# An mLSTM and convolution layer in fp32: the sample states' small products regrouped from pairs to fours, the chunk update in 257 columns, the head loops written out

## The chip, the core and the metric

The kernel runs on one core of one Trainium2 chip. The metric is the device time of one execution in microseconds. A core has TensorE for matrix products (PE, with its weight loads listed as PEld), VectorE (DVE), ScalarE (ACT), GpSimd (POOL) and SyncE (SP), which issues most DMA transfers. The engines run their own instruction streams and wait for each other by semaphores. Operands lie in an on-chip memory of 128 partitions; results of TensorE land in eight accumulator banks (out takes four of them; B4, B5, B6 and B7 are the others). The chip was seen to grant TensorE one of two clocks, 1.2 or 2.4 GHz; the profile gives it as a share of the full one.

## What is computed

One layer over 16 meta tokens and 512 prompt frames of a new stream and 8 x 16 frames of eight running streams (the "samples"), 656 columns in all. A projection of the 1024 channels gives, for each of four heads, 256 channels each of query, key, value and output gate, and the two inputs of a gated convolution branch. The part that the change touches is the chunked matrix memory. Each head runs five chunks of the prompt (16 and four times 128 frames in this kernel; the samples count as chunk 5) with a carried 256 x 256 state, and the eight samples with a state of their own each:

```python
a = b + m0[..., None]
w_state = jnp.exp(a - m)
w_intra = jnp.exp(dmat - m[..., None])
p = w_intra * jnp.einsum('bhtd,bhsd->bhts', q, k)
num = jnp.einsum('bhts,bhse->bhte', p, v) + w_state[..., None] * jnp.einsum('bhed,bhtd->bhte', C0, q)
den = jnp.sum(p, axis=-1) + w_state * jnp.einsum('bhd,bhtd->bht', n0, q)
h = num / jnp.maximum(jnp.abs(den), jnp.exp(-m))[..., None]
C1 = w_last[..., None, None] * C0 + jnp.einsum('bhs,bhse,bhsd->bhed', ws, v, k)
n1 = w_last[..., None] * n0 + jnp.einsum('bhs,bhsd->bhd', ws, k)
```

The heads' outputs are normalised, multiplied by the output gate and projected (the branch); the convolution branch is a depthwise convolution of 31 taps, a layer norm and a projection; both are gated, merged and projected, and a feed-forward block follows. All is fp32, and the states C and n of prompt and samples are outputs too.

## The kernel before

**Weight tiles.** To keep fp32 accuracy every weight tile and its right-hand side are split into a high and a low part, and TensorE forms three products. One tile of 128 output channels is one `gemm` (L374): 8 channel blocks x 3 products x 2 halves of 328 or 320 columns, 48 matmuls. For tile n, SP loads the weights to a ring of four (`ST`), ACT writes the high part (`hi`, `WH`, L325) once tile n-2 is done, DVE subtracts it (`lo`, `WL`, L329), and the gemm of tile n waits for `w_lo`. ACT then evacuates tiles (L659).

**Heads.** A head is twelve tiles, r = 0 to 11: two each of k, q, v, o and four of the convolution's gate and input. After four heads come 16 tiles of gates and branch (the "GM tiles", j = 0, 1, ...), and further stages which the change leaves alone. Right after tile r=1 of a head, TensorE transposes the normalised output of the head before (`headnorm_out`), and POOL, DVE and ACT turn it into the next operand (`epilogue_out`, `epilogue_gate`).

**Slots.** The matrix-memory work of a head stands in 14 slots on TensorE: slot 0 after tile r=7, slots 1 and 2 inside tile r=8 after 16 and 32 of its 48 matmuls, slot 3 after it, and so on to slot 12 after r=11, and 13. Tables by slot number say what stands where: `S_SLOT` (scores of chunk c, "S"), `NUM_SLOT` (numerator of c, and the update of the carried state "U" with chunk c), `TR_SLOT` (the four 128-column transposes of one sample's state, "T"), `READ_SLOT` (the product of a pair of sample states with its queries, "R") and `PAIR_SLOT` (the pair's state update, "D"). All of these are plain fp32 matmuls at L1580 (`mm`) and L1575 (`tr`); the trace holds each of them as two records. A read uses tiles of 32 output columns (128*32 in the trace), an update tiles of 32 rows (32*128), two tiles of the array at a time. In U the 256 columns of the state and the column of the normaliser are separate products (L1750 and L1752). Banks: transposes and reads in B4, scores in B5, numerators in B6, updates in B7 (a pair's second sample in B6).

**The other engines.** DVE and ACT run in program order through the same slots: DVE multiplies scores by weights (`p_ready`), adds updates to states (`update`, L1033: two a pair, `c1`; for U `ct_ready`), takes statistics of a chunk's output (`stats`), and runs `conv_input`. In heads 1 to 3 it also runs the 62 convolution taps of the head before, two instructions each (L1033, CV<-WK,cwu,CV), so many after each tile and slot by the tables `CONV_TILE` and `CONV_SLOT`. ACT copies turned states (`c0t_ready`, two buffers), copies reads and numerators, and issues the DMAs of the sample states: `c1_store` (L724), `c0_load` (L717) and, in `states_in`, the load of n (L777) and of the first four states of a head. PE's code is written out for all heads. On SP (L511), ACT (L885) and DVE (its end is L1372) head 0 is written out and heads 1 to 3 are a hardware loop.

Names in the rows: WK is the work area in which q, k, tokens by frame, states and their products lie; CV holds the convolution's output and one of the buffers for turned states; sm, mv and bst are small statistics; n0b is the samples' n; GH and GL are high and low part of the gated head output.

Of the kernel before, what the change touches and what calls it, by code (L numbers as in the profile page):

```python
# [25 lines left out]
D = 1024  # L26
# [55 lines left out]
UPDATES = []  # L82
for _s in range(NSLOT):
    if _s in NUM_SLOT and NUM_SLOT[_s] < NPC:
        UPDATES.append(("U", NUM_SLOT[_s]))
    if _s in PAIR_SLOT:
        UPDATES.append(("D", PAIR_SLOT[_s]))
# [3 lines left out]
STORE_SLOT = {_s + 1: _p for _s, _p in PAIR_SLOT.items()}  # L91
LOAD_SLOT = {_s + 2: _p + 2 for _s, _p in PAIR_SLOT.items() if _p < 2}


def pairs_done(s):
    return 2 * sum(x < s for x in PAIR_SLOT)
# [8 lines left out]
def build(nc, a):  # L105
    def sb(name, shape, dt=F32):
# [10 lines left out]
    sizes = [("q", 2 * T), ("k", 2 * T), ("qw", 2 * T), ("vn", 6 * 257), ("so", 2 * T), ("kt", 6 * 256),  # L117
             ("vt", 6 * 257), ("vws", 2 * 257), ("c0", C0RING * 512), ("c0t", 514),
             ("pt", 2 * P), ("bc", 2 * T), ("ct", 2 * 257), ("up", 2 * (PAD + TP + NB * (PAD + LB))),
             ("qm", 2 * NB * 24)]  # L120
# [7 lines left out]
    def wk(o, n):  # L128
        return WK[:, o:o + n]
# [5 lines left out]
    num = wk(off["vn"], 6 * 257).rearrange("p (c e) -> p c e", c=6)  # L135
# [46 lines left out]
    c0t = [x.rearrange("p (j e) -> p j e", j=2) for x in (CVF[:, 6 * T2:6 * T2 + 514], wk(off["c0t"], 514))]  # L182
# [64 lines left out]
    def n0_of(i, b):  # L247

        return n0t[:, :, :].rearrange("p j (b h) -> p h j b", h=HEADS)[:, bass.ds(i, 1), :, b:b + 1].rearrange(
            "p o j b -> p (o j) b")  # L250

# [193 lines left out]
    with nc.Block() as block:  # L445

        @block.sync
        def _(sp):
# [28 lines left out]
            def head_loads(i):  # L477
                first = isinstance(i, int)
# [3 lines left out]
                for r, col in enumerate(cols):  # L482
# [6 lines left out]
                    elif r == 3 and not first:  # L489

                        gated = sp.snap(ofcount(n + -1) + 1)
                        tile, src = sp.snap((i - 1) * 2), d_rows[bass.ds(i, 1), :, :]
                        tile1 = sp.snap((i - 1) * 2 + 1)
                        sp.wait_ge(sem("rows_out"), 32)
                        sp.wait_ge(sem(f"of{(n + -1).par % 2}"), gated)
                        bc_load(src)
# [3 lines left out]
                        for x, tl in enumerate((tile, tile1)):  # L500
# [9 lines left out]
            head_loads(0)  # L510
            with sp.Fori(1, HEADS) as i:  # L511
                head_loads(i)
# [58 lines left out]
        def _(g):  # L571
# [34 lines left out]
            g.wait_ge(sem("of0"), N_GM0 // 2 + 1)  # L606
            g.tensor_tensor(ln[0], CV[:, 0, :], CV[:, 1, :], ALU.add).then_inc(sem("csum"), 1)
# [17 lines left out]
        def _(act):  # L625
# [120 lines left out]
            def epilogue_out(i):  # L746

                act.wait_ge(sem("t_ct"), i + 1)
                act.wait_ge(sem("t_int"), 4 * i + 4)
# [36 lines left out]
            def head(i):  # L786

                n = N(N_HEADS0, PER_HEAD, i)
                first = isinstance(i, int)
# [9 lines left out]
                if not first:  # L799
                    states_in(i)  # L800
# [4 lines left out]
                if not first:  # L805
                    exp_weights(i)
                    epilogue_out(i - 1)
# [31 lines left out]
                else:  # L839
                    values_tok(i)  # L840
                hi(n + 8)
                evac(n + 7, two(so[:, 1, NMETA:T]), ACT.Sigmoid)
                if first:
                    values_tok(i)
                for s in range(NSLOT):
                    if s in (1, 4, 7, 10):
                        hi(n + (8 + (s - 1) // 3 + 1))
                    if s in TR_SLOT:
                        b = TR_SLOT[s]
                        act.wait_ge(sem("t_c0"), NB * i + b + 1)  # L850
                        wait(act, "t_int", 4 * i + b // 2)
# [1165 lines left out]
```

## Time and profile before

| | us |
|---|---|
| median of 3 runs | 1280.85 (1280.24 to 1281.9) |
| the profiled execution, own time | 1281.44 |
| its span | 1279.7 |
| PE busy | 1246.7 (97%) |
| PEld busy | 1160.3 (91%) |
| DVE busy | 740.0 (58%) |
| ACT busy | 390.1 (30%) |
| POOL busy | 19.8 (2%) |
| chain that ended last | PE 92%, issue 3%, ACT 2%, DVE 2% |
| DMA, mean | 91 GB/s |

The time is that of the whole execution; the span runs from the first to the last instruction in the trace, so 1.7 us lie around it. Busy shares are means over the stages. A matmul's record ends later than the next one begins, because matmuls are pipelined; the pace is read from starts. The mean granted clock was .991.

### The profile page before, as it was taken

To read this page: it belongs to the slowest core of one execution; us is meant where nothing else is said; L and a number is where in the kernel's file an instruction comes from. 1 tells how busy PE (TensorE), PEld (TensorE's weight loads), DVE (VectorE), ACT (ScalarE), POOL (GpSimd) and SP (SyncE) were. 2 spreads that over 40 slices of the span, in tenths; PEclk is the share of its full clock that TensorE was granted. 3 is DMA by queue.
4 is the path that set the end of the run, shared out by engine and by line. 5 is a ranking of instruction groups with operands and counts; after the bars stand their busy time and mean duration, and the time that the engine had idled before them with its cause. 6 is when DMAs were issued, how large, how long until landed. Compare 5 with 4: busy or idle time off the path is not lost.

```text
span 1279.7 us, 19762 instructions
## 1 busy us (share of the span) xinstructions
PE 1246.7 (97%) x7760; PEld 1160.3 (91%) x7760; DVE 740.0 (58%) x1311; ACT 390.1 (30%) x562; POOL 19.8 (2%) x37
## 2 busy tenths in 40 slices
PE   7999999989998999999999999999999999999997
PEld 7998899879987998899999998899899889989986
DVE  5633469857985798899755565443243333323453
ACT  4442243223322332231236533233123213312431
POOL 1000000000000000200000000000000000000000
PEclk8999999999999899999999999999999999999999
DMA  8253162334333423352332335012322222222221
GB/s 230 71 154 99 50 163 69 97 96 116 71 96 96 117 66 101 89 79 79 75 82 67 99 106 180 28 50 83 99 66 83 82 72 77 82 68 81 83 82 50
DMA packets 160541, 116.38 MB, mean 91 GB/s; under 512 B 13887, under 2 KB 148247, under 8 KB 160450
## 3 DMA queue, kind: packets, MB, share of 16 engines
q1 hardware_dynamic: 139122, 94.58, 27.2%
q10 hardware_dynamic: 21328, 20.55, 5.1%
q8 instruction: 62, 1.02, 0.3%
q14 instruction: 29, 0.24, 0.1%
HBM read 100.89 MB, written 14.21 MB: 90 GB/s over the span
## 4 chain that ended last, share of the span: by engine, by line
PE 92%; issue 3%; ACT 2%; DVE 2%; DVEq 0%; POOLq 0%; POOL 0%
PE out L374 42%; PE out L1580 29%; PE bank L1580 17%; PE bank L1575 4%; DVE WK L1033 1%; ACT CV L627 1%; PE out L382 1%; DVE WK L1030 0%; DVE WL L329 0%; ACT WH L325 0%; ACT L659 0%; ACT L627 0%; ACT GH L627 0%; DVE XL L1030 0%; ACT WK L659 0%
## 5 line engine op out<-in xcount | busy, mean ns | idle before, releaser
L329 DVE TENSOR_TENSOR WL<-ST,WH 128x1024 fp32r<-128x1024 f32 x137 | 168.2, 1228 | 180.7 <-ACT WH L430 100.6
L374 PE MATMUL out<-XH,WH 128*128 128x320 f32 (+1 forms) x1024 | 241.4, 317 | 9.0 <-DVE WL L329 9.0
L374 PE MATMUL out<-XH,WL 128*128 128x320 f32 (+1 forms) x1024 | 238.7, 314 | 0.0
L374 PE MATMUL out<-XL,WH 128*128 128x320 f32 (+1 forms) x1024 | 238.2, 314 | 0.0
L1033 DVE SCALAR_TENSOR_TENSOR CV<-WK,cwu,CV 128x512 f32 (+1 forms) x480 | 227.1, 541 | 0.6
L374 PEld LDWEIGHTS out<-XH,WH 128*128 128x128 f32 x1024 | 173.1, 190 | 10.3 <-DVE WL L329 9.6
L374 PEld LDWEIGHTS out<-XL,WH 128*128 128x128 f32 x1024 | 173.3, 190 | 4.6 <-issue 4.4
L374 PEld LDWEIGHTS out<-XH,WL 128*128 128x128 f32 x1024 | 173.1, 189 | 2.9 <-issue 2.7
L1030 DVE TENSOR_TENSOR WK<-WK 128x640 f32<-128x640 f32 (+7 forms) x86 | 65.1, 770 | 109.5 <-ACT WK L996 100.2
L1580 PE MATMUL out<-XH,WL 128*128 128x320 f32 (+2 forms) x512 | 119.9, 310 | 0.0
L1580 PE MATMUL out<-XL,WH 128*128 128x320 f32 (+2 forms) x512 | 119.6, 310 | 0.0
L1580 PE MATMUL out<-XH,WH 128*128 128x320 f32 (+2 forms) x512 | 119.4, 309 | 0.0
L325 ACT ACTIVATE WH<-ST 128x1024 fp32r<-128x1024 f32 x81 | 85.3, 1053 | 90.2 <-PE out L374 59.5
L1580 PE MATMUL bank<-WK 32*128 32x256 f32 (+6 forms) x536 | 99.9, 353 | 6.8 <-DVE WK L1033 6.8
L430 ACT ACTIVATE WH<-ST 128x1024 fp32r<-128x1024 f32 x56 | 58.9, 1052 | 135.3 <-PE bank L1580 68.9
L659 ACT ACTIVATE WK<-out 128x640 f32<-128x640 f32 (+1 forms) x56 | 39.8, 710 | 188.7 <-PE out L374 181.2
L1580 PEld LDWEIGHTS bank<-WK 128*128 128x128 f32 (+3 forms) x536 | 69.1, 179 | 21.6 <-issue 15.6
L1580 PEld LDWEIGHTS out<-XH,WH 128*128 128x128 f32 x512 | 86.3, 188 | 1.0
L1580 PEld LDWEIGHTS out<-XL,WH 128*128 128x128 f32 x512 | 86.3, 188 | 0.7
L1580 PEld LDWEIGHTS out<-XH,WL 128*128 128x128 f32 x512 | 86.2, 188 | 0.7
L627 ACT ACTIVATE WK<-bank 128x512 f32<-128x512 f32 (+5 forms) x100 | 43.0, 467 | 73.1 <-PE bank L1580 71.4
L1575 PE MATMUL bank<-ident,WK 128*128 128x128 f32 (+6 forms) x427 | 58.0, 275 | 6.3 <-DVE WK L1033 5.4
(219 smaller groups left out, 1608.4 us busy)
## 6 DMA issues: line engine op xcount, KB each, us to landing
ST<-in_w_in SPq DMA_DIRECT2D x65, 512.0 KB, 4.1
ST<-in_w_ff SPq DMA_DIRECT2D x64, 512.0 KB, 4.0
WK<-in_state_mlstm_C ACTq DMA_DIRECT2D x32, 256.0 KB, 3.0
o_C_sample<-WK ACTq DMA_DIRECT2D x32, 256.0 KB, 2.4
WK<-in_x_prompt SPq DMA_DIRECT2D x8, 512.0 KB, 6.4
ST<-in_w_branch_m SPq DMA_DIRECT2D x8, 512.0 KB, 4.0
ST<-in_w_branch_c SPq DMA_DIRECT2D x8, 512.0 KB, 4.1
ST<-in_w_out SPq DMA_DIRECT2D x8, 512.0 KB, 3.5
```

The costliest lines, as they stand in the source:

```text
L325: act.activation(WH[:, par % 2, :, :], ST[:, par % NSTAGE, :, :], ACT.Copy).then_inc(sem("w_hi"), 1)
L329: dve.tensor_tensor(WL[:, par % 2, :, :], ST[:, par % NSTAGE, :, :], WH[:, par % 2, :, :].bitcast(F32), ALU.subtract).then_inc(sem("w_lo"), 1)
L374: last = pe.matmul(out[s][:, h, 0:H], w[:, s, kk, :], x[:, kk, h * H:(h + 1) * H], start=(m < 2), stop=(m >= len(ms) - 2))
L382: last = pe.matmul(out[0][:, h, 0:HALF], w[:, 0, kk, :], x[:, kk, h * HALF:(h + 1) * HALF], start=(kk == 0 and w is WH and x is XH), stop= ...
L430: act.activation(WH[:, n.par % 2, :, :], ST[:, n.par, :, :], ACT.Copy).then_inc(sem("w_hi"), 1)
L627: act.activation(o, i, fn, **kw).then_inc(sem(name), 1)
L659: act.activation(o, gout(n), fn, **kw).then_inc(sem(f"of{n.par % 2}"), 1)
L1030: return dve.tensor_tensor(o, x, y, op)
L1033: return dve.scalar_tensor_tensor(o, x, s, y, op0, op1)
L1575: ins = pe.transpose(o, i, ident[0:r, 0:r])
L1580: return pe.matmul(o, l, r, start=start, stop=stop)
```

## The change

1. The eight samples of a head are worked in two rounds of four in place of four pairs. A read is eight matmuls, four tiles of 32 columns into the four row groups of B4; an update eight matmuls, four tiles of 32 rows into four banks (B6, B7, B5, B4). Turned states have four buffers in place of two. The second round's update stands in the new slot 14, in the middle of the next head's tile r=0 (after the last head: of GM tile 0); two transposes stand in new slots -2 and -1 inside tile r=7. DVE adds a round in four instructions; the second round after the normalisation of the head's output in the next head. The four stores of a round and the loads of the next four states are issued together by ACT, the stores of the second round after `hi` of the next head's tile r=2; `states_in` moves from there to behind `hi` of r=3.
2. U is two products of 257 columns (B7 and the upper part of B5), and DVE's update two instructions of 257 columns.
3. The tables of slots and taps change with it (the numerators and scores one slot later, from chunk 1 or 2 on), and `slot` is split into named functions.
4. The loops over heads on SP, ACT and DVE are written out. The buffer `num` loses its unused row; POOL waits for the last numerator before it writes into that area.

```diff
-S_SLOT = {2: 1, 4: 2, 6: 3, 8: 4, 10: 5}
-NUM_SLOT = {1: 0, 3: 1, 5: 2, 7: 3, 9: 4, 13: 5}
-PAIR_SLOT = {2: 0, 4: 1, 8: 2, 12: 3}
-TR_SLOT = {0: 0, 1: 1, 3: 2, 4: 3, 7: 4, 8: 5, 10: 6, 11: 7}
-READ_SLOT = {2: 0, 5: 1, 9: 2, 12: 3}
+S_SLOT = {2: 1, 5: 2, 7: 3, 9: 4, 11: 5}
+NUM_SLOT = {1: 0, 4: 1, 6: 2, 8: 3, 10: 4, 13: 5}
+ROUND_SLOT = {3: 0, 14: 1}
+READ_SLOT = {2: 0, 12: 1}
+TURN_SLOT = {-2: [0], -1: [1], 0: [2], 1: [3], 8: [4], 9: [5], 10: [6], 11: [7]}
+TURN_SLOT0 = {**TURN_SLOT, -2: [], -1: [0], 0: [1, 2]}
-CONV_SLOT = {s: 2 if s % 2 else 3 for s in range(NSLOT) if 0 < s < 12}
+CONV_SLOT = {1: 2, 2: 3, 4: 1, 5: 4, 6: 3, 7: 3, 8: 3, 9: 3, 10: 2, 11: 3}
...
-            head_loads(0)
-            with sp.Fori(1, HEADS) as i:
+            for i in range(HEADS):
                 head_loads(i)
...
                 hi(n + 2)
                 if not first:
-                    states_in(i)
+                    round_store(i - 1, 1)
                 evac(n + 1, two(k[:, 1, :]), scale=DH ** -0.5)
...
                 hi(n + 3)
                 if not first:
+                    states_in(i)
                     exp_weights(i)
                     epilogue_out(i - 1)
...
-                    for x in range(2):
-                        b = 2 * c + x
...
+                    for x in range(4):
+                        col = 23 + SAMPLE[4 * c + x]
+                        dve.wait_ge(sem(f"c0_in{x}"), 16 * (2 * i + c + 1))
+                        stt(c0[:, x, :, :], c0[:, x, :, :], colH[:, col:col + 1],
+                            round_bank(x).rearrange("p (j e) -> p j e", j=2), ALU.mult, ALU.add).then_inc(sem("c1"), 1)
...
             head(0)
-            with dve.Fori(1, HEADS) as i:
+            for i in range(1, HEADS):
...
                 if j == 0:
                     epilogue_norm(HEADS - 1)
+                    update(HEADS - 1, NUPD - 1)
...
+            def read_states(i, r):
+
+                pe.wait_ge(sem("c0t_ready"), NB * i + 4 * r + 4)
+                pe.wait_ge(sem("qw_ready"), i + 1)
+                for j in range(2):
+                    for g in range(4):
+                        ins = mm(B4[32 * g:32 * g + 32, 0:257], qm[:, j, g, LB * r:LB * r + 2 * LB],
+                                 c0t[g][:, j, :], j == 0, j == 1)
+                ins.then_inc(sem("t_int"), 1)
...
+                for e in range(2):
+                    for g in range(4):
+                        rows = slice(32 * g, 32 * g + 32)
+                        ins = mm(round_bank(g)[:, e * DH:e * DH + DH], w[rows, e * P:e * P + P], ktok[rows, SMP, :])
+                ins.then_inc(sem("t_upd"), 1)
...
+            def numerator(i, c):
...
+                pe.wait_ge(sem("p_ready"), 5 * i + c)
+                wait(pe, "num", 5 * i + c - 1)
+                if c == 1:
+                    pe.wait_ge(sem("c1"), NB * i + 4)
...
-                        for j in range(2):
-                            mm(B5[:, 384 + j:385 + j], ktok[0:L, c, j * P:j * P + P], w[0:L, DH:DH + 1])
-                        for j in range(2):
-                            ins = mm(B7[:, j * DH:j * DH + DH], ktok[0:L, c, j * P:j * P + P], w[0:L, 0:DH])
+                for j in range(2):
+                    ins = mm((B7[:, 0:257], B5[:, P:P + 257])[j], ktok[0:L, c, j * P:j * P + P], w)
+                ins.then_inc(sem("t_upd"), 1)
```

On PE, before, slots 12 and 13 at the end of a head read and update the last pair, and then form the samples' numerator. (`bank` are B4 to B7; `32x257` is a read, `128x256` an update, the last `128x257` the numerator.)

```order
L1580 MATMUL bank<-CV,WK 32x257 [waits c0t_ready]
L1580 MATMUL bank<-WK 32x257
L1580 MATMUL bank<-CV,WK 32x257
L1580 MATMUL bank<-WK 32x257
L1580 MATMUL bank<-WK 128x256 [waits n1,ct_ready,vws]
L1580 MATMUL bank<-WK 128x256 x3
L1580 MATMUL bank<-WK 128x257 [waits c1,n1,num,p_ready]
L374 MATMUL out<-XH,WH 128x328 [waits of1,w_lo]
```

The same place after:

```order
L1576 MATMUL bank<-WK 32x257 [waits qw_ready,c0t_ready]
L1576 MATMUL bank<-WK 32x257
L1576 MATMUL bank<-CV,WK 32x257 x2
L1576 MATMUL bank<-WK 32x257 x2
L1576 MATMUL bank<-CV,WK 32x257 x2
L1576 MATMUL bank<-WK 128x257 [waits n1,num,p_ready]
L372 MATMUL out<-XH,WH 128x328 [waits of1,w_lo]
```

The update has left the place ahead of the numerator, and with it the numerator's wait for `c1`. The update's eight matmuls follow inside the next tile:

```order
L372 MATMUL out<-XH,WH 128x328 x2
L372 MATMUL out<-XL,WH 128x328 x2
L372 MATMUL out<-XH,WL 128x328 x2
L1576 MATMUL bank<-WK 128x256 [waits p_ready,all_samples,ct_ready,num,vws]
L1576 MATMUL bank<-WK 128x256 x7
L372 MATMUL out<-XH,WH 128x328 x2
```

Behind slot 3, which updates the first round, PE has a third of tile r=9 (16 matmuls) and then slot 4, whose numerator now waits for `c1`:

```order
L1576 MATMUL bank<-WK 128x256 [waits p_ready,ct_ready,first_samples,vws]
L1576 MATMUL bank<-WK 128x256 x7
L372 MATMUL out<-XH,WH 128x328 [waits of0,w_lo]
L372 MATMUL out<-XH,WH 128x328
...
L372 MATMUL out<-XL,WH 128x328 x2
L1576 MATMUL bank<-WK 128x257 [waits c1,ct_ready,num,p_ready]
L1576 MATMUL bank<-WK 128x257 x2
L1576 MATMUL bank<-WK 128x257 [waits vws]
```

On DVE, before, a head of the loop ends with the sum and the statistics of the samples' numerator and the branch back to the `lo` of the next head:

```order
L1030 TENSOR_TENSOR WK<-out,WK 128x184
L1030 TENSOR_TENSOR WK<-out,WK 128x328
L1030 TENSOR_TENSOR WK<-WK,bank 128x257
L1254 BN_STATS bst<-WK 128x6
L1372 REGISTER_ALU
L1372 COMPARE_AND_BRANCH
```

After, the next head's `lo` (`WL<-ST,WH`) follows without a branch, and behind the normalisation (its last five instructions are `WK<-WK,sm`) stands the second round's state update:

```order
L1254 BN_STATS bst<-WK 128x6
L327 TENSOR_TENSOR WL<-ST,WH 128x1024
L1035 SCALAR_TENSOR_TENSOR sm<-WK 128x5
L1032 TENSOR_TENSOR sm<-sm,colH 128x5
...
L1184 TENSOR_SCALAR WK<-WK,sm 128x256 x5
L1035 SCALAR_TENSOR_TENSOR WK<-WK,colH,bank 128x512 x4
L1204 COPY colH<-colA 128x31
```

On ACT, after, the five loads of `states_in` (L772, L712) stand between `hi` of r=3 and the step that leads to GH, the head output's high part; before, they stood one `hi` earlier:

```order
L323 ACTIVATE WH<-ST 128x1024 [waits tile_done,ld0]
L772 DMA n0b<-in_state_mlstm_n 8x256 [waits n1_out]
L712 DMA WK<-in_state_mlstm_C 128x2x256 [waits c1_out0]
L712 DMA WK<-in_state_mlstm_C 128x2x256 [waits c1_out1]
L712 DMA WK<-in_state_mlstm_C 128x2x256 [waits c1_out2]
L712 DMA WK<-in_state_mlstm_C 128x2x256 [waits c1_out3]
...
L622 ACTIVATE WK<-bank 128x512 [waits t_int,t_ct]
L747 DMA o_C_prompt<-WK 128x2x256 [waits cp_sb]
L749 DMA o_n_prompt<-WK 128x2x1
L622 ACTIVATE GH<-WK 128x1280 [waits hmf]
```

## Rows read from the trace of the kernel before

**Rows 1.** PE's waits: engine, line, whom for; us in total, times, longest

```profile
PE out L374 <- DVE WL L329: 9.5, 4, 4.6
PE bank L1580 <- DVE WK L1033: 6.8, 4, 1.7
...
PE bank L1575 <- ACT WK L627: 1.0, 1, 1.0
```

**Rows 2.** PE timeline, tiles r=0 and r=1: start us, us, engine, line, operands, count, [idle before]

```profile
289.48 0.57 PE L374 MATMUL out<-XH,WH 128*128 128x328 f32 x2 [4.37 <-DVE WL L329]
...
404.83 0.67 PE L1580 MATMUL bank<-WK 128*128 128x257 f32 x2 [1.71 <-DVE WK L1033]
...
405.64 0.46 PE L374 MATMUL out<-XL,WH 128*128 128x328 f32 x2
...
412.25 0.47 PE L374 MATMUL out<-XH,WL 128*128 128x328 f32 x2
417.36 0.91 PE L374 MATMUL out<-XH,WH 128*128 128x328 f32 x2 [4.65 <-DVE WL L329]
```

**Rows 3.** DVE timeline behind the loop's branch, head 2 to head 3

```profile
416.08 1.22 DVE L329 TENSOR_TENSOR WL<-ST,WH 128x1024 fp32r<-128x1024 f32 x1 [9.19 <-issue]
```

**Rows 4.** Stretches: us, busy PE PEld DVE ACT POOL (count), PEclk, DMA share, GB/s

```profile
289.48:298.36 8.88, 8.88 (x49) 8.87 (x50) 6.86 (x31) 1.76 (x3) 0.00 (x0) 0.81 0.77 202
417.36:427.41 10.05, 10.05 (x49) 10.04 (x49) 6.87 (x31) 1.75 (x3) 0.00 (x0) 0.70 0.72 205
346.00:405.50 59.50, 57.79 (x380) 50.25 (x379) 49.05 (x108) 13.77 (x29) 0.00 (x0) 1.00 0.25 75
```

**Rows 5.** PE timeline, slot 2 of head 2: read, scores, update, next gemm

```profile
353.55 0.40 PE L1580 MATMUL bank<-CV,WK 128*32 128x257 f32 x1
353.55 0.40 PE L1580 MATMUL bank<-WK 128*32 128x257 f32 x1
...
354.54 0.71 PE L1580 MATMUL bank<-WK 128*128 128x128 f32 x4
...
355.18 1.13 PE L1580 MATMUL bank<-WK 32*128 32x256 f32 x8
...
356.24 0.57 PE L374 MATMUL out<-XL,WH 128*128 128x328 f32 x2
```

**Rows 6.** PE timeline, slot 3 of head 2: numerator and U, next gemm

```profile
359.19 2.78 PE L1580 MATMUL bank<-WK 128*128 128x257 f32 x14
361.62 0.65 PE L374 MATMUL out<-XH,WH 128*128 128x328 f32 x2
```

**Rows 7.** DVE timeline, slots 2 to 6 of head 2

```profile
356.48 1.41 DVE L1033 SCALAR_TENSOR_TENSOR WK<-WK,colH,bank 128x512 f32<-128x512 f32 x2 [0.90 <-PE bank L1580]
...
362.01 0.88 DVE L1033 SCALAR_TENSOR_TENSOR WK<-WK,colH,bank 128x2 f32<-128x2 f32 x2 [0.84 <-PE bank L1580]
...
363.40 1.92 DVE L1033 SCALAR_TENSOR_TENSOR CV<-WK,cwu,CV 128x512 f32 x4
...
366.38 0.28 DVE L1030 TENSOR_TENSOR WK<-bank,WK 128x128 f32<-128x128 f32 x1
...
378.99 1.02 DVE L1030 TENSOR_TENSOR WK<-out,WK 128x128 f32<-128x128 f32 x4
```

**Rows 8.** ACT's DMA issues of four sample states, written-out code of head 0

```profile
79.82 1.96 ACTq L717 DMA_DIRECT2D WK<-in_state_mlstm_C  x4
```

**Rows 9.** DVE timeline ahead of tile r=4 of head 2, then PE's start of it

```profile
305.48 1.49 DVE L1030 TENSOR_TENSOR GL<-WK,GH 128x1280 f32 x1 [2.16 <-ACT GH L627]
...
313.15 1.22 DVE L329 TENSOR_TENSOR WL<-ST,WH 128x1024 fp32r<-128x1024 f32 x1
...
315.79 0.55 PE L374 MATMUL out<-XH,WH 128*128 128x328 f32 x2
```

**Rows 10.** DVE timeline ahead of GM tile 2, then PE's start of it

```profile
546.24 1.23 DVE L329 TENSOR_TENSOR WL<-ST,WH 128x1024 fp32r<-128x1024 f32 x1
...
548.43 0.45 PE L374 MATMUL out<-XH,WH 128*128 128x320 f32 x2
```

More of the change, by code:

```diff
@@ L90 @@
 C0RING = 4
[L91 to L96, printed above, removed]
+STORE_SLOT, LOAD_SLOT = 5, 6
 CONV_TILE = {2: 7, 3: 4, 4: 7, 5: 7, 6: 7, 7: 3}
-CONV_SLOT = {s: 2 if s % 2 else 3 for s in range(NSLOT) if 0 < s < 12}
+CONV_SLOT = {1: 2, 2: 3, 4: 1, 5: 4, 6: 3, 7: 3, 8: 3, 9: 3, 10: 2, 11: 3}
 TAPS = 2 * CONV_W
@@ L250, in n0_of, with round_bank, turn_bank @@
             "p o j b -> p (o j) b")
+    def round_bank(g):
+        return (B6, B7, B5, B4)[g]
+    def turn_bank(i, b):
+        return B7 if i == 0 and b == 2 else B6 if b < 4 else B4
     def gout(n):
@@ L877, in head, with turned, round_store @@
                               ).then_inc(sem("n1_out"), 16)
+            def turned(i, s):
+                for b in (TURN_SLOT if i else TURN_SLOT0).get(s, []):
+                    act.wait_ge(sem("t_c0"), NB * i + b + 1)
+                    wait(act, "t_int", 2 * i + b // 4)
+                    if b == 0:
+                        wait(act, "cp_out", 16 * i)
+                    act.activation(c0t[b % 4][:, :, DH:DH + 1], n0_of(i, SAMPLE[b]), ACT.Copy)
+                    copy(c0t[b % 4][:, :, 0:DH], turn_bank(i, b).rearrange("p (j e) -> p j e", j=2), "c0t_ready")
+            def round_store(i, r):
+                for x in range(4):
+                    c1_store(i, 4 * r + x)
             def numer(i, c):
@@ L881, in numer @@
                 act.wait_ge(sem("t_num"), 5 * i + c)
-                copy(num[0:L, c, :], B6[0:L, 0:257], "num")
-            head(0)
-            with act.Fori(1, HEADS) as i:
+                copy(num[0:L, c - 1, :], B6[0:L, 0:257], "num")
+            for i in range(HEADS):
                 head(i)
@@ L1682, in slot, with turn @@
+            def turn(i, s):
+                for b in (TURN_SLOT if i else TURN_SLOT0).get(s, []):
+                    bank = turn_bank(i, b)
                     if b == 0:
                         pe.wait_ge(sem("kv_tok"), 8 * i + 8)
-                    wait(pe, "c0t_ready", NB * i + b)
-                    if b in (2, 4):
-                        pe.wait_ge(sem("first_samples"), 2 * i + b // 2)
-                    if b == 6:
-                        pe.wait_ge(sem("all_samples"), 2 * i + 1)
@@ new lines, in update_chunk @@
+            def update_chunk(i, c):
+                u = UPDATES.index(("U", c))
+                L = CHUNKS[c][1]
+                w = vws[0:L, (NUPD * i + u) % 2, :]
+                pe.wait_ge(sem("vws"), NUPD * i + u + 1)
+                if c == 0:
+                    wait(pe, "cp_sb", i)
+                    pe.wait_ge(sem("kv_tok"), 8 * i + 8)
+                    if i == 0:
+                        pe.wait_ge(sem("c0t_ready"), 3)
+                for j in range(2):
+                    ins = mm((B7[:, 0:257], B5[:, P:P + 257])[j], ktok[0:L, c, j * P:j * P + P], w)
+                ins.then_inc(sem("t_upd"), 1)
@@ L1718, in slot @@
+            def slot(i, s):
+                turn(i, s)
+                if s in READ_SLOT:
+                    read_states(i, READ_SLOT[s])
+                if s in S_SLOT:
+                    scores(i, S_SLOT[s])
                 if s == 11:
@@ L1770, in head @@
                         xh, xl = (XH2, XL2) if r in FRAMES_ONLY else (XH, XL)
-                        gemm(pe, n + r, xh, xl)
+                        gaps = []
+                        if r == 0 and not first:
+                            gaps = [lambda: slot(i - 1, 14)]
+                        if r == 7:
+                            gaps = [(lambda: values_by_frame(i)) if first else (lambda: slot(i, -2)), lambda: slot(i, -1)]
+                        gemm(pe, n + r, xh, xl, gaps=gaps)
                     else:
```

272 lines of the change are left out of this document (114 added, 158 removed).

## The prediction, made before the changed kernel had run

> **What bounds the kernel now.** I read the page's busy shares and the chain of waits first. PE is busy almost throughout and the chain runs through it, so a gain must either take work off PE or take away one of its waits. The list of PE's waits says which there are [rows 1]: 9.5 us in four waits for a low part of weights from DVE, of which the largest is 4.6, and 6.8 us in four waits, one a head, for a DVE update. The rest of PE's idle time before the heads' end lies in the kernel's first stage, which the change does not touch. The timeline puts places to them. The two long waits for `lo` are the starts of tile r=1 in heads 2 and 3, and the waits of 1.7 us are the samples' numerator in slot 13 [rows 2]. Then I read the slots themselves, because there the change takes matmuls away [rows 5, 6], and DVE and ACT around them, because their slack decides what the shorter slots are worth [rows 7 to 9].
>
> **The loops written out.** Ahead of the `lo` for which tile r=1 waits, DVE is idle for 9.19 us and the trace names no releaser, only "issue" [rows 3]. The instruction before it is the branch at the loop's end. So the wait belongs to the loop's return, and it comes on the two returns (heads 2 and 3) and nowhere in straight code. PE loses 4.37 and 4.65 us [rows 2]. It loses more behind that: matmuls follow each other by (412.25-405.64)/44 = .150 us [rows 2], so a tile of 48 takes 7.21, but the two tiles r=1 took 8.88 and 10.05, with granted clocks of .81 and .70 of full [rows 4]. The clock fell to its lower level in them after PE had stood still. That is 1.67 + 2.84 = 4.5 us. I take all of it as gained: 9.0 + 4.5 = **13.5**. The lower bound is 0, if straight code stalls as long at that place (a rival). SP's and ACT's loops cost PE nothing that the waits show, and I credit nothing for them.
>
> **The slot-13 wait.** Before, the last update and the numerator stand next to each other, and the numerator waits until DVE has emptied the bank. After, this update stands in the middle of the next tile and the numerator does not wait for it: 4 x 1.71 = **6.8** [rows 1, 2]. Next late there would be the numerator's inputs, the scores of slot 11, which lie more than a tile's third back; I see no new wait. The 1.0 us wait of a transpose for ACT in head 0 [rows 1] belongs to a turn that moves behind more cover: **1.0**.
>
> **Matmuls.** A read of a pair takes 354.54-353.55 = .99 us, an update 356.24-355.18 = 1.06 [rows 5]. Two tiles start at the same printed time, so the eight records run as four steps. If four tiles do the same, a round costs what a pair costs, and there are two rounds for four pairs: 2 x .99 + 2 x 1.06 = 4.1 us a head, **16.4** in four heads. This is the term with the widest bounds, 0 (four tiles run two at a time) to 16.4, and below 0 if they run one at a time; both are rivals. The row of two tiles at a time is the nearest there is, and nothing in it suggests that two is the limit: even the two starts of one step have no printed distance. U has four products of which two have one column. Numerator and U together take 361.62-359.19 = 2.43 us for 14 records [rows 6]; without the four records of one column ten wide ones are left, nine steps and the last one, which the gemm follows almost at once. A step is .25 at most (a read's .99 over four, with the change of shape at its end) and about .22 without that change: 1.98, so the U saves .45 (.2 with the larger step), x 20 updates = **9.0** (4 to 9). So matmuls give 25.4. The three new breaks inside gemms (slots -2, -1, 14) and the breaks that go about cancel; what one costs is at most the difference of the first gemm steps behind a slot and plain ones, some .1, so 1 us stays in the bounds.
>
> The Trainium skill, "TensorE: Matmul & The Clock Gate", Part 3, "Measured speedup vs the span model", gives 3.07 for four row tiles and 2.38 for three column tiles, not 4 and 3. By it a step of four would cost some 1.3 times a full one, an estimate: 1.23 us a head, and the forecast would be 5 us later. Two tiles in this trace show the full factor of two; four at a time are in no row.
>
> Gains: 13.5 + 6.8 + 1.0 + 25.4 = **46.7**.
>
> **New waits.** Now DVE has less time between the slots, and I went through them for what ends last.
> - Slot 4 (all heads): the numerator waits for the four additions of the first round, slot 3. Counted from the update's start PE arrives after 1.06 + 16 x .150 = 3.5 us. DVE starts 356.48-355.18 = 1.30 after that start, needs 1.41 for two additions and so 2.8 for four [rows 5, 7], and its signal takes another .24 (the update's end to the DVE start, 356.24 to 356.48): 4.3. Wait .7 to .8, x 4 = **2.8**. Behind PE in that wait stands the U of chunk 1, and all that follows.
> - Slot 8 (heads 1 to 3): the numerator of chunk 3 needs the weighted scores. Behind the U of slot 6 DVE has its update, the next weighting and statistics (363.40-362.01 = 1.39), three taps (six instructions at 1.92/4, 2.8), the convolution input (1.0), a `lo` (1.2) and the weighting (.28) [rows 3, 7], 6.7 with some of it overlapped; with the signal 6.7 to 6.9. PE has two thirds of a tile, 4.8, and a score and a turn of four records each (at most 355.18-354.54 = .64 each, rather .45 [rows 5]): 5.7 to 6.1. Wait .6 to 1.2, I take 1.0, x 3 = **3.0**.
> - Tile r=4 (heads 1 to 3): `states_in` now stands ahead of the copy of the head output to GH. Its four state loads take ACT 1.96 us to issue [rows 8], and DVE has already waited 2.16 for GH; `lo` of r=4 ended 1.42 before PE needed it (313.15 + 1.22 against 315.79) [rows 9]. So 1.96 - 1.42, about .6, x 3 = **1.8**. No queue is lengthened: the loads are the same ones.
> - GM tile 2: the second round's update, four additions or 2.8 us, stands ahead of its `lo`, which had .97 to spare (546.24 + 1.23, 548.43) [rows 10]: **1.8**. In heads 1 to 3 the same update stands after the `lo` of r=1, where DVE has a tile's length.
>
> Waits: 2.8 + 3.0 + 1.8 + 1.8 = **9.4**; bounds 0 (DVE has idle time that closes up) to twice that. ACT's stores and loads four at a time, SP's straight code and POOL's wait cost nothing: ACT is busy 13.77 of 59.5 us in the slots [rows 4], and the load of the next four states is issued some 14 us ahead of its turn.
>
> **Sum.** 46.7 - 9.4 = 37.3. Against the profiled execution, 1281.44, that is 1244.1; the median of the runs lies .59 below that execution, so **1243.5**. With waits of 0 it is 1234, with twice the waits 1253.
>
> **Rivals.**
> 1. Four tiles run as two pairs, so the change does not do what it says: the 16.4 us come back, **1260**. For it: no row shows more than two tiles at a time. Against it: the two show no cost of sharing.
> 2. DVE sets the pace of the slots. In the stretch of tiles r=8 to r=11 of head 2 it is busy 49.05 of 59.5 us [rows 4]. The second round's additions leave the stretch (2.8), so it keeps 46.3, and PE's stretch shrinks to about 52 by the terms above. If DVE's idle time of 10.45 stayed, because it always comes from waiting for the next slot and cannot be shifted, the stretch would be 56.7: 4.7 x 3 heads = 14, **1257**. For it: DVE's waits for PE in this stretch are many and short [rows 7]. Against it: these waits are on PE, and end earlier when PE is earlier.
>    The Trainium skill, "TensorEngine Tiling (Array Packing)", "PSUM Bottleneck", says that after such a speedup the emptying of the banks may become the bound, and to use both engines for it; here the additions of both rounds stay on DVE alone. The waits that I expect at slot 4 are of that kind.
> 3. DVE's stall of 9 us stays in straight code, since what comes after the seam is code that has not run before either way: 13.5 back, **1257**. Against it: no such gap stands in head 0's straight code, between heads or in the GM tiles, nor where the loop is left after head 3.
> 4. The other side: four tiles are run one after the other. A round would be 16 steps of .25 (the .99 over four), 4.0 us a read and 4.2 an update, two of each: 16.4 a head against 8.2 before and 4.1 in the forecast, so +49, **1292**, slower than before. It decides once a read or update of four costs more than about 3.4 us in place of 1.0. Against it stand the two reads that start at one time [rows 5].
>
> **How the numbers follow.** The forecast, 1234 to 1253 with 1243.5 as its value, gets .69; rival 1 .10, rival 2 .08, rival 3 .07, rival 4 .04; .02 lie below 1234, if DVE's earlier starts also take away waits that I did not count. The range goes from 1233 to 1259, which takes in the forecast with rivals 2 and 3, .84, and leaves out rivals 1 and 4 and what is below. Some 0.2% (2.6 us) is what a measurement can tell from no change; all cases but rival 4 are faster by far more. Faster .95, the same .01 (rival 4 in part), slower .04.
>
> **What the profile after would show.** The timeline at tile r=1 of heads 2 and 3 should have no idle time and a full clock (the stretch of 48 matmuls 7.2 us). A read or an update of four should take about 1.0 us with four records at one start. In PE's list the waits of slot 13 should be gone, and small ones stand at the numerators of slots 4 and 8 (L1576 for DVE), the gemm of r=4 (L372 for DVE's `lo`) and GM tile 2. If reads take 2 us it is rival 1; if DVE's idle time in the slots is as long as before and PE waits at most slots, rival 2; if the idle time ahead of `lo` stays, rival 3. I would be wrong in the sum if the new waits hit at more slots than I went through, the turns in r=7 above all, which now need ACT's copies earlier.

## The result, and the profile after

The changed kernel takes 1239.35 us (median of 4 runs, 1239.09 to 1240.54) against 1280.55 before (median of 4, 1279.13 to 1281.9): a ratio of 0.968 (95% interval 0.9663 to 0.9697), 41.2 us faster. The forecast was 1243.5 in a range of 1233 to 1259. The profiled execution took 1239.42 (span 1237.7), 42.0 less than before. PE is busy 1214.8 us of the span, 98%.

PE's waits after (engine, line, whom for; us in total, times, longest) answer to [rows 1]. The 9.5 and 6.8 us are gone, and so is head 0's 1.0 us wait for ACT. The three rows are new: slot 8 (0.9 in each of heads 1 to 3), GM tile 2 (1.6, with two small ones) and slot 4 (0.4 each).

```profile
PE bank L1576 <- DVE WK L1032: 2.7, 3, 0.9
PE out L372 <- DVE WL L327: 2.1, 3, 1.6
...
PE bank L1576 <- DVE WK L1035: 1.3, 3, 0.4
```

The four tiles of a read, of head 2 (PE timeline), against [rows 5]: sixteen records in four steps, 332.39-331.38 = 1.01 us for four samples where two took .99. The update of four takes 336.52-335.44 = 1.08 where a pair's took 1.06.

```profile
331.38 0.41 PE L1576 MATMUL bank<-WK 128*32 128x257 f32 x2
331.40 0.41 PE L1576 MATMUL bank<-CV,WK 128*32 128x257 f32 x2
...
332.06 0.38 PE L1576 MATMUL bank<-WK 128*32 128x257 f32 x2
332.08 0.39 PE L1576 MATMUL bank<-CV,WK 128*32 128x257 f32 x2
332.39 0.71 PE L1576 MATMUL bank<-WK 128*128 128x128 f32 x4
...
335.44 1.15 PE L1576 MATMUL bank<-WK 32*128 32x256 f32 x16
336.52 0.42 PE L372 MATMUL out<-XH,WH 128*128 128x328 f32 x1
```

Three stretches (us, busy time of PE, PEld, DVE, ACT, POOL, then PEclk, DMA share, GB/s), against [rows 4]: tile r=1 of heads 2 and 3, to the start of r=2 and with `headnorm_out` in them, and the slots of head 2. The clock is at its full level in all three.

```profile
268.48:277.14 8.66, 8.66 (x64) 8.65 (x63) 4.65 (x14) 2.91 (x4) 0.00 (x0) 1.00 0.89 257
383.22:391.88 8.66, 8.66 (x65) 8.65 (x63) 4.64 (x14) 2.91 (x4) 0.00 (x0) 1.00 0.95 273
324.68:374.54 49.86, 48.52 (x332) 43.62 (x330) 43.24 (x97) 12.92 (x26) 0.00 (x0) 1.00 0.25 72
```

At the seam of heads 2 and 3 on DVE (timeline; [rows 3] before), the low part follows the last statistics with no idle time; the branch is gone and with it the 9 us:

```profile
376.06 0.43 DVE L1254 BATCH_NORM_STATS2 bst<-WK 128x6 f32<-128x256 f32 x1
376.40 1.21 DVE L327 TENSOR_TENSOR WL<-ST,WH 128x1024 fp32r<-128x1024 f32 x1
```

PE's tiles can be compared one by one, since a tile of either kernel takes the same time to .03 us wherever nothing was changed. Then the gain is where it was looked for. From r=0 to the start of r=2, heads 2 and 3 got 3.26 + 1.66 and 3.53 + 2.83 us shorter, although r=0 now holds an update of 1.28. From r=7 to r=11 head 0 got 10.55 us shorter and each other head 7.97, although r=7 got .89 longer there by the two turns that moved into it. Head 1's r=0 and GM tile 0 got 1.28 and 1.27 longer by the new update, GM tiles 1 and 2 1.72 and .12 by the wait between them. Together that is 41.3 us less. The other .5 of the difference between the two profiles lie in the first stage, which the change leaves alone.

### The profile page after: what moved, and what is told of

Same layout as the page of the kernel before. It is cut to its first block, busy times and chain, and to the rows that moved or that the text cites. A ratio compares the mean times of both kernels' runs of the same rounds, so it can differ in the third digit from the quotient of the medians.

```text
span 1237.7 us, 18596 instructions
## 1 busy us (share of the span) xinstructions
PE 1214.8 (98%) x7680; PEld 1137.6 (92%) x7680; DVE 734.8 (59%) x1299; ACT 388.4 (31%) x558; POOL 20.9 (2%) x37
## 4 chain that ended last, share of the span: by engine, by line
PE 91%; DVE 4%; ACT 2%; issue 2%; DMA 1%; DVEq 0%; SPq 0%; POOLq 0%; POOL 0%
PE out L372 42%; PE out L1576 30%; PE bank L1576 15%; PE bank L1571 4%; DVE WK L1035 1%; DMA WK<-in_x_prompt 1%; ACT CV L622 1%; DVE CV L1035 1%; PE out L380 1%; DVE WL L327 1%; DVE WK L1032 0%; ACT L622 0%; ACT WH L323 0%; ACT L654 0%; ACT GH L622 0%
## 5 line engine op out<-in xcount | busy, mean ns | idle before, releaser
L1035 DVE SCALAR_TENSOR_TENSOR CV<-WK,cwu,CV 128x512 f32<-128x512 f32 x480 | 227.2, 546 | 0.1
L1576 PE MATMUL bank<-WK 128*128 128x257 f32 (+4 forms) x456 | 75.0, 372 | 4.3 <-DVE WK L1032 2.7
L1576 PEld LDWEIGHTS bank<-WK 128*128 128x128 f32 (+3 forms) x456 | 52.6, 177 | 18.5 <-issue 9.7
L622 ACT ACTIVATE WK<-bank 128x512 f32<-128x512 f32 (+6 forms) x96 | 41.6, 472 | 76.4 <-PE bank L1576 72.7
```

The source lines that it names most:

```text
L622: act.activation(o, i, fn, **kw).then_inc(sem(name), 1)
L1035: return dve.scalar_tensor_tensor(o, x, s, y, op0, op1)
L1576: return pe.matmul(o, l, r, start=start, stop=stop)
```

## The experiments

**The loops, and slot 13.** Two kernels start from the kernel before. The first has DVE's head loop written out, the second SP's and ACT's as well.

```diff
-                first = isinstance(i, int)
+                first = i == 0
...
-            with dve.Fori(1, HEADS) as i:
+            for i in range(1, HEADS):
```

> The kernel before with the loop over heads 1 to 3 written out on DVE alone; SP and ACT keep theirs. Theory (the loop's return on DVE makes the stall, and nothing else): the waits of 4.37 and 4.65 us for WL at tile r=1 of heads 2 and 3 go, and with them the slow tiles behind them (8.88 and 10.05 us in place of 7.21). Against the kernel after, tiles r=0 and r=1 of heads 2 and 3 are longer by 3.26 + 1.66 and 3.53 + 2.83 us, and the kernel after has an update of 1.28 us in each r=0, so 13.8 us in all: 1280.5 - 13.8 = 1266.7. Rival 3 of the prediction (straight code stalls as long at this place): 1280.5, with DVE idle for about 9 us ahead of that low part. A further rival (ACT's or SP's return is nearly as late and takes the place): between 1267 and 1280, with PE waiting at the same tile.

> The kernel before with the loops over heads written out on SP, ACT and DVE. Theory (only DVE's return reaches PE): the same time as with DVE's alone, 1266.7, within 1 us. Rival (the loops on SP and ACT hold something back that shows once DVE is straight): faster than with DVE's alone by more than 2 us.

Measured: 1273.08 and 1272.95 (before 1281.34). SP's and ACT's loops cost nothing, as expected, but DVE's gave 8.3 and not 13.8. The waits at r=1 are gone, with no idle time of DVE there, so no rival holds. The time came back elsewhere: stretches of the first, from slot 13's end through r=0 of heads 2, 3, GM and head 1 (columns as above):

```profile
277.50:287.10 9.60, 9.29 (x50) 9.15 (x51) 7.56 (x31) 2.55 (x3) 0.00 (x0) 0.82 0.86 239
400.60:410.10 9.50, 9.30 (x51) 9.15 (x51) 7.47 (x30) 2.55 (x3) 0.00 (x0) 0.82 0.93 248
523.60:532.90 9.30, 9.11 (x50) 8.96 (x51) 8.02 (x19) 1.06 (x1) 7.38 (x5) 0.82 0.56 161
155.60:164.10 8.50, 7.72 (x50) 7.70 (x51) 7.79 (x31) 2.55 (x3) 0.00 (x0) 1.00 0.67 176
```

The same 1.71 us wait stands in slot 13 ahead of each. Behind three of the four the granted clock fell to its lower level for a while, and tile r=0 took 8.88, 8.76 and 8.48 us in place of 7.41, 7.41 and 7.21: 4.1 us. In the profiled execution of the kernel before it fell behind none of these four waits. In the second kernel it fell behind two, and in that with the chunk update alone (below) behind three.

Two more kernels were made to tell this apart. In one, slot 13's numerator has a bank of its own and needs no wait; the other has this and DVE's loop written out.

```diff
-                if s == 11 or s in NUM_SLOT:
+                if s == 11 or s in NUM_SLOT and s != 13:
                     wait(pe, "c1", NB * i + pairs_done(s))
...
-                        ins = mm(o, pt[:, c % 2, :], vtok[:, c, :])
+                        ins = mm(B5[:, 0:257], pt[:, c % 2, :], vtok[:, c, :])
...
-                tt(num[:, SMP, :], num[:, SMP, :], B6[:, 0:257], ALU.add).then_inc(sem("num"), 1)
+                tt(num[:, SMP, :], num[:, SMP, :], B5[:, 0:257], ALU.add).then_inc(sem("num"), 1)
```

> The kernel before, where the samples' numerator in slot 13 goes to bank B5 and not to B6, so that it needn't wait for DVE's additions of the last pair; loops stay. The four waits of 1.71 us go: 6.8 us less, 1274.4, if they cost only themselves. Theory (a wait of 1.7 us can also let the granted clock fall for a few us behind it, as it did in three of four heads once DVE's loop was written out): in the profiled execution of the kernel before the clock fell behind none of the four, so here 6.8 and no more, and the two falls behind the 4 us waits of tile r=1 stay. Rival (the 1.7 us come back in the next tile, whose weights are late): less than 4 us.

> The kernel before with both edits: DVE's head loop written out, and slot 13's numerator in B5. Theory (the loop's stall is worth 13.8 us; written out alone it gave 8.2, because the clock then fell behind slot 13's waits, in three heads for 4.1 us in all; without these waits there is nothing left behind which it falls): 13.8 + 6.8 = 20.6 us less, 1260.7, and the granted clock at its full level from tile r=0 of head 0 to the end. Rival (the 5 us that the written-out loop fell short are lost in another way, and stay lost): 8.2 + 6.8 = 15.0 less, 1266.3, with falls of the clock at other places.

Measured: 1278.01 for the numerator alone, 3.9 us less than before (1281.88; ratio 0.9975, 0.9964 to 0.9986) where my theory had 6.8, and 1261.36 for both, 20.5 less, as its theory had it. So the parts gave 8.3 and 3.9, and together 20.5. In the first of the two, slot 13's waits are gone, 1.75 us in each head, but those for the low part are longer in total and one by one, and DVE's idle time is about as before, 9.27 us where it was 8.92 (waits and PE timeline, then DVE timeline, of that kernel):

```profile
PE out L374 <- DVE WL L329: 12.9, 4, 6.5
```

```profile
288.59 0.64 PE L374 MATMUL out<-XH,WH 128*128 128x328 f32 x1 [6.47 <-DVE WL L329]
...
287.31 1.23 DVE L329 TENSOR_TENSOR WL<-ST,WH 128x1024 fp32r<-128x1024 f32 x1 [9.27 <-issue]
```

PE comes to r=1 earlier, and DVE's stall ends when it ended before, or a little later. So r=0 of heads 2 and 3, which last until that wait ends, got 2.1 and 1.3 us longer, and two of the four gains were given back almost in full. This is my rival for that run ("less than 4"), with r=1 and not r=0 as the place. With both waits away, r=0 of heads 2, 3 and GM runs at the full clock, 7.41 us for the first two:

```profile
274.70:282.11 7.41, 7.41 (x51) 7.38 (x50) 6.56 (x25) 2.55 (x3) 0.00 (x0) 1.00 0.74 201
394.37:401.78 7.41, 7.41 (x51) 7.38 (x49) 6.59 (x25) 2.55 (x3) 0.00 (x0) 1.00 0.71 194
514.00:521.30 7.30, 7.30 (x51) 7.26 (x50) 7.17 (x17) 1.06 (x1) 4.25 (x3) 1.00 0.67 182
```

The prediction's 13.5 + 6.8 = 20.3 is thus shown as a sum, but neither term is to be had alone.

**The chunk update alone**, in the kernel before: two products of 257 columns and DVE's additions to match.

```diff
-                            mm(B5[:, 384 + j:385 + j], ktok[0:L, c, j * P:j * P + P], w[0:L, DH:DH + 1])
-                        for j in range(2):
-                            ins = mm(B7[:, j * DH:j * DH + DH], ktok[0:L, c, j * P:j * P + P], w[0:L, 0:DH])
+                            ins = mm((B7[:, 0:257], B5[:, P:P + 257])[j], ktok[0:L, c, j * P:j * P + P], w[0:L, :])
```

> The kernel before with only the chunk update changed: two products of 257 columns, and two DVE instructions of 257 columns. Theory (the one-column products cost PE their records and nothing hides them): 20 updates of .45 us, 9.0 us less: 1271.5. Rival (the next thing on PE waits for DVE's additions, which have two instructions of 257 columns now in place of one of 512 and one of 2, some .4 us longer): less than half of it, 1276 or more, with new waits of PE for DVE at the slots behind an update.

Measured: 1273.43 (before 1281.34), 7.9 less. Tile by tile the four heads' r=8 to r=10 got 2.17 us shorter each, 8.7 in all or .43 an update, against .45 forecast. Otherwise the heads differ where the clock fell at other waits than before: head 1's r=0 took 1.56 us more and head 3's r=1 2.73 less. No new wait for DVE appeared in the heads.

**Four tiles.** Two kernels start from the kernel after. In one the products of a read are issued sample by sample, and those of an update in the same way; in the other the third and fourth sample use the array's places of the first two.

```diff
-                for j in range(2):
-                    for g in range(4):
+                for g in range(4):
+                    for j in range(2):
                         ins = mm(B4[32 * g:32 * g + 32, 0:257], qm[:, j, g, LB * r:LB * r + 2 * LB],
```

> The kernel after, with the eight products of a read and of an update issued sample by sample (both products of the first sample, then of the second, and so on) and not across the four samples. Same work, same banks, same waits. Theory (tiles run at the same time when they stand next to each other, and TensorE starts matmuls in the order of issue): the second product of one sample runs beside the first of the next, so five steps of two records in place of two steps of two, 10 x .217 against 4 x .217: 1.3 us for each of 16 reads and updates, 20.8 us: 1260. Rival a (the array reorders, so the order of issue does not matter): no change, 1239.4. Rival b (neighbours don't overlap unless their products are alike): 16 records one after another, 12 x .217 x 16 = 42 us more: 1281.

Measured: 1240.22, no change: rival a, and my theory fell. The read of that kernel (PE timeline) starts the CV tiles, the third and fourth sample, .02 us behind the first, although all four products of the first two (WK) are issued ahead of them:

```profile
331.39 0.42 PE L1576 MATMUL bank<-WK 128*32 128x257 f32 x2
331.41 0.42 PE L1576 MATMUL bank<-CV,WK 128*32 128x257 f32 x2
331.63 0.39 PE L1576 MATMUL bank<-WK 128*32 128x257 f32 x2
331.65 0.39 PE L1576 MATMUL bank<-CV,WK 128*32 128x257 f32 x2
```

The other kernel's edit of the read, whose products now also go pair by pair, and of the rows of the update:

```diff
-                for j in range(2):
-                    for g in range(4):
-                        ins = mm(B4[32 * g:32 * g + 32, 0:257], qm[:, j, g, LB * r:LB * r + 2 * LB],
+                for j, g in [(j, g + x) for g in (0, 2) for j in range(2) for x in range(2)]:
+                        ins = mm(B4[32 * (g % 2):32 * (g % 2) + 32, 0:257], qm[:, j, g, LB * r:LB * r + 2 * LB],
...
-                        rows = slice(32 * g, 32 * g + 32)
+                        rows = slice(32 * (g % 2), 32 * (g % 2) + 32)
```

> The kernel after, but the four tiles of a read and of an update stand at two places of the array in place of four (samples 2 and 3 of a round at the columns and rows of 0 and 1). The same number and shape of matmuls; the third and fourth sample's results overwrite the first two's and the second half of the rows is not used, so part of the result is left out. Theory (tiles run beside each other by their place in the array): eight steps for four, 4 x .217 = .87 us more in each of 16 reads and updates, 13.9 us: 1253. Rival (small tiles follow each other faster wherever they stand): no change, 1239.4.

Measured: 1254.0, 14.7 more. A read takes eight steps (341.17-339.31 = 1.86 us where it took 1.01), and each of the sixteen reads and updates costs PE .85 more, 13.6 in all:

```profile
339.31 1.06 PE L1576 MATMUL bank<-WK 128*32 128x257 f32 x8
340.20 1.04 PE L1576 MATMUL bank<-CV,WK 128*32 128x257 f32 x8
341.17 0.71 PE L1576 MATMUL bank<-WK 128*128 128x128 f32 x4
```

The update keeps its order and its four banks, and tile r=0, which holds an update alone, got .85 longer like the others; so neither the order nor results that share a place account for it. What makes four run at once is their place in the array, not their order.

**The loads moved behind one copy more.** The kernel after, with `states_in` back behind the copy of r=2.

```diff
                     round_store(i - 1, 1)
+                    states_in(i)
...
-                    states_in(i)
                     exp_weights(i)
```

> The kernel after, where ACT issues the loads of n and of the four states of the next head behind the low tile's copy of r=2 again, as before (behind the stores that they wait for), and not one copy later, ahead of the head output's GH. The prediction had 1.8 us for the later place: 1237.6 if it was right. Theory from the trace after (ACT's queue issues these DMAs while ACT still runs the evacuation and the copy ahead of them; tile r=4's low part still ends .98 us before PE needs it): no change, 1239.4. Rival (the loads now stop ACT until the stores have landed, and its next copies are late): slower by 1 us or more.

Measured: 1240.22; no tile from the heads on differs from the kernel after by .1 us. ACT's timeline at this place, of the kernel after (ACTq is its queue, which issues DMAs):

```profile
275.90 0.72 ACT L654 ACTIVATE WK<-out 128x656 f32<-128x656 f32 x1 [5.55 <-PE out L372]
275.99 0.31 ACTq L772 DMA_DIRECT2D n0b<-in_state_mlstm_n  x1
276.34 0.39 ACTq L712 DMA_DIRECT2D WK<-in_state_mlstm_C  x1
276.51 1.05 ACT L323 ACTIVATE WH<-ST 128x1024 fp32r<-128x1024 f32 x1
276.77 1.65 ACTq L712 DMA_DIRECT2D WK<-in_state_mlstm_C  x3
278.45 1.28 ACT L622 ACT_TABLE_LOAD   x1 [0.89 <-issue]
```

Of the issues' 2.4 us, 1.5 lie beside the evacuation and the copy that ACT is still running; ACT stands idle for .89. Tile r=4's low part has .98 to spare in this kernel (DVE, then PE timeline of the kernel after), and 1.86 in the one with the loads moved back:

```profile
290.95 1.22 DVE L327 TENSOR_TENSOR WL<-ST,WH 128x1024 fp32r<-128x1024 f32 x1
...
293.15 0.55 PE L372 MATMUL out<-XH,WH 128*128 128x328 f32 x2
```

**The three new waits**, taken away one by one and together, in the kernel after. Slot 4: the numerator waits for the one addition that empties its bank. Slot 8: DVE weights chunk 3's scores ahead of the low part. GM: the last additions behind the low part.

```diff
                 if c == 1:
-                    pe.wait_ge(sem("c1"), NB * i + 4)
+                    pe.wait_ge(sem("c1"), NB * i + 1)
...
+                if c == 1:
+                    pe.wait_ge(sem("c1"), NB * i + 3)
                 if c == 0:
                     wait(pe, "cp_sb", i)
```

```diff
-                    if s in (1, 4, 7, 10):
-                        lo(n + (8 + (s - 1) // 3 + 1))
                     if s in S_SLOT:
...
+                    if s in (1, 4, 7, 10):
+                        lo(n + (8 + (s - 1) // 3 + 1))
```

```diff
                     epilogue_norm(HEADS - 1)
+                if j == 1:
                     update(HEADS - 1, NUPD - 1)
-                if j == 1:
```

> The kernel after, where the numerator of chunk 1 (slot 4) waits for the first of the round's four additions alone (its bank is B6), and the chunk update behind it for the first three (its banks are B7 and B5). Theory (the wait for the fourth addition is what stops PE in slot 4): PE arrives 3.5 us after the update's start, the first addition ends some 2.2 us after it and the third 3.6 us after it, when the chunk update is still 1.4 us away; the wait goes. Slot 4 cost .68 us more than slot 6, whose products are the same, in heads 1 to 3 and .52 in head 0: 2.6 us less, 1236.8. Rival (something else, the scores' weights, ends as late): no change, 1239.4.

> The kernel after, where DVE weights the scores of chunk 3 ahead of the low part of tile r=11 (slot 7), not behind it. Theory (in heads 1 to 3 the numerator of slot 8 waits for the last of a DVE row of work, of which the low part is 1.2 us): of the 1.16 us that slot 8 costs beyond slot 10 with the same products, all or nearly all goes, 3 x 1.0 to 3 x 1.16: 3.0 to 3.5 us less, 1236.1. The low part, which had 5.7 us to spare, is late for nobody. Rival (the taps and the convolution's input ahead of it are enough to hold it up): half of it or less, 1238.

> The kernel after, where DVE does the last head's second round of state additions behind the low part of GM tile 2, not ahead of it. Theory (those four additions make the wait of 1.56 us at that tile): 1.7 us less, 1237.6, and the next users of these states (stores, and the transposes of the head's output in that tile) have room. Rival (the wait moves on to the transposes in the middle of GM tile 2, which wait for the additions): no change, 1239.4.

> The kernel after with the three edits at once: slot 4's waits by bank, slot 8's weighting ahead of the low part, the last additions behind the low part of GM tile 2. Theory (the three waits lie at different places of PE's chain and add up): 2.6 + 3.3 + 1.7 = 7.6 us less, 1231.8. Rival (removing one makes the next place wait): less than the sum of the three measured alone, by more than 1 us.

Measured: 1237.39, 1236.27 and 1238.24, and 1232.82 together (ratio to the kernel before 0.9619, 0.9604 to 0.9633): 2.0, 3.1, 1.1 and 6.5 us less than the kernel after had in its own runs. The profiles are sharper than the medians, because the first stage, which no edit touches, took from 31.2 to 32.5 us in these profiles. Slot 4's tiles got .71 shorter in heads 1 to 3 and .52 in head 0 (2.65), slot 8's 1.13 to 1.14 in heads 1 to 3 (3.4), GM tile 1 1.72. In the kernel with all three edits these are the same numbers at the same places, and only GM tile 4 got longer, by .2; PE's list has no wait of more than .3 us in the heads any more. The mechanisms are those forecast: of slot 8, DVE's row of work and PE's start in the kernel after show it (timelines),

```profile
353.69 1.03 DVE L1032 TENSOR_TENSOR WK<-out,WK 128x128 f32<-128x128 f32 x4
354.63 1.22 DVE L327 TENSOR_TENSOR WL<-ST,WH 128x1024 fp32r<-128x1024 f32 x1
355.76 0.28 DVE L1032 TENSOR_TENSOR WK<-bank,WK 128x128 f32<-128x128 f32 x1
...
356.10 0.48 PE L1576 MATMUL bank<-WK 128*128 128x257 f32 x1 [0.90 <-DVE WK L1032]
```

and of GM tile 2 these, ended by the low part that stood behind the additions:

```profile
502.57 2.72 DVE L1035 SCALAR_TENSOR_TENSOR WK<-WK,colH,bank 128x512 f32<-128x512 f32 x4
505.21 1.22 DVE L327 TENSOR_TENSOR WL<-ST,WH 128x1024 fp32r<-128x1024 f32 x1
...
506.48 0.57 PE L372 MATMUL out<-XH,WH 128*128 128x320 f32 x2 [1.56 <-DVE WL L327]
```

This last kernel is the fastest of all, 6.5 us ahead of the kernel after.

## Why the prediction was right, and where it was off

- **The loops (13.5).** 4.54 + 1.66 in head 2 and 4.81 + 2.83 in head 3, with the new update in r=0 taken out: 13.8. Right within the whole change. As a term by itself it was not: 8.3 alone, because the clock toll went to other waits. The prediction had tied the 4.5 us of clock to the stall at r=1; in the runs the clock also fell behind the waits in slot 13. That the term came out whole is in part luck: the prediction added the two waits up and did not see that each is worth its price only if the other goes too, and the change happened to take both.
- **Slot 13 (6.8).** Gone in full (1.75 a head), but worth 3.9 with the loop left in, since the head's next wait is set by DVE. Head 0's 1.0 us wait for ACT is gone too.
- **Matmuls (25.4).** The four tiles run as the row of two said, with no price of sharing, so rivals 1 and 4 fall (1260, 1292). The gain by tiles, once the new waits are added back, is 27.3 us: U 8.7 (forecast 9.0), and reads and updates 18.6 (16.4). Of the 18.6, width gives 13.6 by the run with two places (.85 for each of 16 blocks), and 2.8 are the ends of a block that the prediction had counted with it (.99 and 1.06 against .85). The last 2.2 are the mis-sized part of this term: four of eight blocks in each head are gone, and 2.2 is .14 us for each of them beyond the time from its start to the next start. The update in tile r=0 shows a price of that kind: it took 1.08 and made the tile 1.28 longer. How the 2.2 divide up no run separates.
- **Factors for four tiles.** By those of the Trainium skill, "TensorE: Matmul & The Clock Gate", Part 3, "Measured speedup vs the span model", the prediction put an estimate of some 5 us on this. The trace disagrees: 1.01 us for four samples against .99 for two, and 1.86 for four at two places.
- **New waits (9.4).** Slot 4: 2.65 against 2.8. Slot 8: 3.4 against 3.0. GM tile 2: 1.7 against 1.8. Tile r=4: none against 1.8, the step that failed. It took 1.96 us of DMA issues as time of ACT, and counted the slack as it stood; but ACT's queue issues beside ACT's own work, so only .89 of it came through, less than the 1.42 that the prediction had to spare.
- **The sum.** 37.3 was forecast and 42.0 measured between the two profiled executions. The 4.7 us between are the r=4 wait (1.8), reads and updates (2.2), the loops (.3), the first stage, which is not touched but ran .5 shorter, and smaller differences, some of them the other way.
- **Rivals 2 and 3** fall. DVE's busy time in head 2's slots went from 49.05 of 59.50 us to 43.24 of 49.86, so its idle time shrank from 10.45 to 6.62: it waits for PE, and PE for it only at slots 4 and 8. And straight code does not stall.

## What to carry to other kernels

A wait's worth is not its length in the list: it is what is left after the next wait on the same engine and after the clock, so two waits in a row should be judged, and removed, together. Small matmuls gained here by standing at different places of the array, in either order of issue that was tried. When an engine gets less cover, go through its order for the one operation that nobody waits for and that stands ahead of one that somebody waits for: two such moves, and one wait narrowed to the addition that it needs, gave 6.5 us more here.

## What the runs showed of the hardware that was not expected

- A standstill of TensorE of 1.71 us was followed by a fall of the clock to its lower level in some cases and not in others: behind none of the four waits in the profile of the kernel before, three of four with DVE's loop written out, two of four with all loops. In these two a fall cost 1.3 to 1.6 us in tile r=0. What decides it no run shows. The kernel before goes from 1278.95 to 1284.54 in 12 runs and the one with neither wait from 1260.71 to 1261.50 in 5, but the one with DVE's loop written out, where these waits stand, only from 1272.90 to 1273.69 in 4; so the scatter can't be put down to them. The Trainium skill, "TensorE: Matmul & The Clock Gate", "What's actually happening", says that the gate's watch runs free of the kernel, so that the same kernel meets it at different points; that would fit a fall behind some waits and not behind others, and is not shown here.
- A wait costs PE more than the idle time in the list, .71 for .44 in slot 4 and 1.13 for .90 in slot 8. In slot 4 the list counts from the end of the last matmul's record, .16 after the next could have started at the pace of .150, and the second matmul behind the wait starts .29 after the first, where the others follow by .217.
- Matmuls at different places of the array can start in another order than they were issued in: issued sample by sample, the third and fourth sample's first products start ahead of the first two's second. The four of a step start some .006 to .014 us apart.
- A backward branch on DVE cost 8.8 to 9.3 us of idle time, on the two returns of a loop of three passes, in the three kernels of this case that keep it; the code that was written out showed none at the same place. The Trainium skill, "Runtime: NRT & Kernel Launch", "Instruction fetch mechanics", has a taken branch out of the fetched window wait for its target to be loaded; the trace agrees as far as that DVE's idle time has no releaser but "issue".
